# PEER gathers: the sums over rows of v, from both table stages to the last one alone

## The chip, the cores and the metric

One core of a Trainium2 chip runs the whole program. The metric is the device time of one execution in microseconds. The kernel before took 1464.52 us (median of three runs, 1464.1 to 1466.99).

## The reference, cut to what matters

The program computes two transformer blocks over 256 tokens of width 1024. The change touches only the last layer, `peer` (a product-key mixture of experts), whose table v is summed as follows:

```python
idx = ...                                  # (T, 8 heads, 16 picks): 128 of 16384 experts per token
g = softmax(top_s)
u_sel = take(u_tab, idx)                   # rows of u, 1024 floats each
h = einsum('bthkd,btd->bthk', u_sel, xb)   # 128 dot products per token
a = gelu(h) * g
y = einsum('bthk,bthkd->btd', a, take(v_tab, idx))   # 128 weighted rows of v per token
x = x + y
```

## The kernel before

The matmuls of all layers work through a list of weight blocks, `ORDER`, each 128 x 1024 floats (512 KB). SyncE fetches every block into `RAW`, a ring of four. The last 256 blocks are the two expert tables: 128 blocks of u (the **u stage**, `UP + c`, c from 0 to 127) and 128 blocks of v (the **w stage**, `WP + c`).

**Two ways to compute the layer.** Tokens 64 to 255 are dense: each goes against all 16384 experts. Tokens 0 to 63 are sparse: only their own 128 experts are fetched, each row by an indirect DMA. A gather takes one row for each of 128 partitions (64 tokens twice), so 64 gathers of u (`("u", j)`) and 64 of v (`("v", j)`) make the 128 picks of a token. Another 16 gathers of u (`("x", k)`) serve 16 of the dense tokens in the u stage.

**The u stage.** TensorE multiplies block c straight from `RAW` in plain float32 (`direct`, L1135, 16 matmul passes of 176 columns), and `gate_matmuls` adds twelve small bf16 matmuls behind 48 of the blocks, the quads. ScalarE takes the gelu of the block's result (`gelu`, L982), which TensorE waits for two blocks later (`pe.wait_ge(s_gel, c - 1)`), and VectorE multiplies by the gates (`gated`, `meet`, L1672). At c = 125 to 127 ScalarE and VectorE also make the first blocks of the w stage. The blocks WP and WP + 1 come into a spare buffer, `OHS` (L510), when the last quads are done, and their two transfers go out in SyncE's queue around block WP - 1.

**The w stage.** Block c is split into a high part `WH` (ScalarE, `high`, L678) and a low part `WL` (VectorE, `low`, L494). TensorE then makes ten matmuls of 512 columns with the activations `GG`. `WH` and `WL` have three buffers, so the engines work about two blocks ahead of TensorE: in step c of their loops they wait until TensorE is done with block c - 1, make `GG` for block c + 2 (ScalarE L1044 and L1045, VectorE L1672), and then split block WP + c + 2. SyncE fetches a block four further on once `WL` of the block in that place is made (`wait_low`).

**The gathers.** GpSimd issues all of them in one list, `TAKEN`, in that order: u gathers go to `UB` (L642) and v gathers to `VB` (L651), three buffers each (`NGET`). A gather waits until VectorE has used the buffer: `pool.wait_ge(s_dot, n - NGET + 1)` for u and `pool.wait_ge(s_vs, j - NGET + 1)` for v. VectorE turns a u row into a dot product (`dot`, L2304) and adds a v row to `YS` (`summed`, L1675 by way of `stt`). Before the first sum of each group of eight it multiplies gelu and gate (`weights`). Which steps of the loops hold them stands in two tables:

```python
TAKE_SLOT = {ROUTED + 1 + 85 * e // (N_SLOT - 1): TAKEN[EARLY_DOTS + e] for e in range(N_SLOT)}   # u stage
SUM_SLOT = {2 + 15 * (j - EARLY_SUMS) // 7: j for j in range(EARLY_SUMS, NSP)}                     # w stage
```

Ten dots are done ahead of step 39 of the u stage. The other 54 dots of u, the 16 of x and 8 sums (`EARLY_SUMS`) stand in 78 of the steps 40 to 125. From step 94 on every fourth of them is a sum (94, 98, 102, 107, 111, 116, 120, 125). The other 56 sums stand in the steps 2 to 119 of the w stage, seven in each fifteen. After the last one ScalarE moves half of `YS` (step 122) and VectorE adds the halves (step 124).

Of the kernel before, what the change touches and what calls it, by code (L numbers as in the profile page):

```python
# [113 lines left out]
NSP = 64  # L114
# [80 lines left out]
NGG = 3  # L195

EARLY_DOTS = 10
EARLY_SUMS = 8
TAKEN = [("u", j) for j in range(EARLY_DOTS)] + [("x", k) for k in range(NX)] + [("u", j) for j in range(EARLY_DOTS, 40)]
for _k in range(EARLY_SUMS):  # L200
    TAKEN += [("u", 40 + 3 * _k), ("u", 41 + 3 * _k), ("u", 42 + 3 * _k), ("v", _k)]
TAKEN += [("v", j) for j in range(EARLY_SUMS, NSP)]
N_SLOT = NSP + NX + EARLY_SUMS - EARLY_DOTS
TAKE_SLOT = {ROUTED + 1 + 85 * e // (N_SLOT - 1): TAKEN[EARLY_DOTS + e] for e in range(N_SLOT)}
# [2 lines left out]
DOTTED = {c: take for c, take in TAKE_SLOT.items() if take[0] != "v"}  # L207
X_DONE = max(c for c, take in DOTTED.items() if take[0] == "x")

SUM_SLOT = {2 + 15 * (j - EARLY_SUMS) // 7: j for j in range(EARLY_SUMS, NSP)}  # L210
GROUP = 8


# [52 lines left out]
def build(nc, wall, par, con, xt, rel, keys, utab, out):  # L266
    ctx = ExitStack()
    with ctx:
# [1401 lines left out]
        def vector_program(dve):  # L1670
# [6 lines left out]
            def low_if_mine(b):  # L1677
                if not low_on_pool(b) and b not in DIRECT:
                    low(dve, b)
# [688 lines left out]
            def summed(j):  # L2368

                if j % GROUP == 0:  # L2370
                    weights(j // GROUP)
                    dve.wait_ge(s_wgt, j // GROUP + 1)
                dve.wait_ge(d_v[j % NGET], 16 * (j // NGET + 1))
                if j == 0:
                    dve.wait_ge(s_xe, 2)
                    dve.wait_ge(s_zero, 2)
                else:
                    dve.wait_ge(s_vs, j)
                stt(YS[:, :], VB[:, j % NGET, :], AS[:, j:j + 1], YS[:, :], ALU.mult, ALU.add).then_inc(s_vs, 1)
# [27 lines left out]
            for c in range(127):  # L2407
                if 1 <= c < 126:
                    activations_low(c + 2)
                if WP + c + 2 < N_BLOCKS:  # L2410
                    low_if_mine(WP + c + 2)
                if c in SUM_SLOT:
                    summed(SUM_SLOT[c])
                if c == 124:
# [159 lines left out]
```

## Time and profile before

| | us |
|---|---|
| median of three runs | 1464.52 |
| the profiled execution | 1466.01 |
| its span | 1463.8 |
| TensorE busy in the span | 1440.5 (98%) |
| VectorE busy | 1128.2 (77%) |
| ScalarE busy | 773.2 (53%) |
| GpSimd busy | 342.2 (23%) |

A busy TensorE is one with a matmul in its pipe. The DMA share is the mean busy share of the core's 16 DMA engines, and it can come out a little over 1 in short stretches. A line number can be that of a helper (`mm`, `tt`, `stt`), so rows are told apart by the buffers that they name.

### The profile page before, as it was taken

The numbers are of one execution on the slowest core, as the hardware profiler recorded it, in microseconds if no ns is written. First come the engines' busy times: TensorE is split into PE (matmuls) and PEld (weight loads), VectorE is DVE, ScalarE is ACT, GpSimd is POOL, SyncE is SP. The second block draws the span as 40 slices with busy tenths as digits, with TensorE's granted clock in tenths as the row PEclk, the third lists the DMA queues.
The fourth block names the chain that finished last, engine by engine and source line by source line (L and its number), as shares of the span: only waits on it lengthen the run. The fifth ranks groups of instructions, "written<-read, shape, count | busy, mean of one in ns | idle before, by whom it ended". The sixth has DMA issues, their size and how long they took to land.

```text
span 1463.8 us, 26213 instructions
## 1 busy us (share of the span) xinstructions
PE 1440.5 (98%) x10046; PEld 1335.7 (91%) x10046; DVE 1128.2 (77%) x2197; ACT 773.2 (53%) x1583; POOL 342.2 (23%) x259
## 2 busy tenths in 40 slices
PE   6999999999999999999999999999999999999998
PEld 6999997789999988899999999999999988888886
DVE  6766678867666686877778797787788788888886
ACT  7555556666555556643455222444444466666665
POOL 1111112301111121201006112323333233333330
PEclk9999999999999999999999999999999999999999
DMA  5666656445665565454555579999999998999996
GB/s 189 194 193 189 188 174 236 151 140 167 187 188 188 183 198 183 140 154 144 171 175 159 164 262 346 343 343 353 362 368 365 341 326 319 337 336 331 320 339 202
DMA packets 98074, 353.06 MB, mean 241 GB/s; under 512 B 10904, under 2 KB 12192, under 8 KB 97952
## 3 DMA queue, kind: packets, MB, share of 16 engines
q1 hardware_dynamic: 77216, 275.90, 56.7%
q0 software_dynamic: 20736, 75.51, 14.0%
q8 instruction: 80, 1.31, 0.4%
q14 instruction: 42, 0.34, 0.1%
HBM read 350.32 MB, written 1.05 MB: 240 GB/s over the span
## 4 chain that ended last, share of the span: by engine, by line
PE 94%; DVE 2%; issue 1%; ACT 1%; POOL 1%; DMA 1%; SPq 0%; ACTq 0%; POOLq 0%; DVEq 0%
PE ps L1105 93%; DVE WL L494 1%; DMA RAW<-wall 1%; PE ps L1307 0%; PE ps L1326 0%; ACT HH L696 0%; POOL FS L587 0%; POOL NR L558 0%; DVE SQN L1672 0%; ACT SQN L685 0%; DMA XT<-xt 0%; POOL WH L567 0%; PE ps L1225 0%; DVE HL L1675 0%; DVE XT L1672 0%
## 5 line engine op out<-in xcount | busy, mean ns | idle before, releaser
L494 DVE TENSOR_TENSOR WL<-RAW,WH 128x1024 fp32r<-128x1024 f32 x359 | 440.7, 1228 | 163.3 <-ACT WH L678 154.4
L678 ACT ACTIVATE WH<-RAW 128x1024 fp32r<-128x1024 f32 x350 | 368.8, 1055 | 240.2 <-PE ps L1105 223.9
L1105 PE MATMUL ps<-XT,RAW 128*128 128x176 f32 x2048 | 317.8, 314 | 1.1 <-DMA RAW<-wall 0.6
L1105 PEld LDWEIGHTS ps<-XT,RAW 128*128 128x128 f32 x2048 | 305.6, 190 | 2.1 <-ACT BIG L976 0.9
L1105 PE MATMUL ps<-HH,WH 128*128 128x256 f32 x976 | 275.4, 282 | 0.8 <-DVE FP L1672 0.5
L1105 PE MATMUL ps<-HL,WH 128*128 128x256 f32 x976 | 272.6, 279 | 0.0
L1105 PE MATMUL ps<-HH,WL 128*128 128x256 f32 x976 | 272.4, 279 | 0.0
L1105 PE MATMUL ps<-WH,GG 128*128 128x512 f32 x768 | 261.9, 395 | 0.0
L1105 PE MATMUL ps<-WL,GG 128*128 128x512 f32 x512 | 202.0, 395 | 0.0
L1105 PEld LDWEIGHTS ps<-HH,WH 128*128 128x128 f32 x976 | 183.5, 188 | 2.2 <-DVE FP L1672 0.7
L1105 PEld LDWEIGHTS ps<-HL,WH 128*128 128x128 f32 x976 | 183.5, 188 | 0.0
L1105 PEld LDWEIGHTS ps<-HH,WL 128*128 128x128 f32 x976 | 183.6, 188 | 0.0
L1105 PEld LDWEIGHTS ps<-WH,GG 128*128 128x128 f32 x768 | 144.7, 188 | 34.0 <-issue 0.4
L651 POOL DMA_INDIRECT VB<-wall,IDXV x64 | 101.0, 1579 | 196.7 <-DVE YS L1675 189.2
L587 POOL TENSOR_TENSOR FS<-FS,RN 128x256 f32<-128x256 f32 x44 | 62.6, 1423 | 280.8 <-ACT FS L742 280.8
L1105 PEld LDWEIGHTS ps<-WL,GG 128*128 128x128 f32 x512 | 96.5, 188 | 22.4
L642 POOL DMA_INDIRECT UB<-utab,IDXU x64 | 66.5, 1040 | 169.4 <-DVE UB L2304 144.3
L1105 PE MATMUL ps<-FH,WH 128*128 128x256 f32 x352 | 98.4, 280 | 0.3 <-DVE WL L494 0.2
L1105 PE MATMUL ps<-FH,WL 128*128 128x256 f32 x352 | 97.8, 278 | 0.0
L1105 PE MATMUL ps<-FL,WH 128*128 128x256 f32 x352 | 97.8, 278 | 0.0
L2304 DVE SCALAR_TENSOR_TENSOR UB<-UB,XS 128x1024 f32<-128x1024 f32 x64 | 78.1, 1221 | 16.1 <-DMA UB<-utab,IDXU 12.6
L1105 PE MATMUL ps<-WH,HH 128*128 128x512 f32 (+1 forms) x208 | 84.7, 407 | 2.5 <-DVE WL L494 2.4
(298 smaller groups left out, 2418.6 us busy)
## 6 DMA issues: line engine op xcount, KB each, us to landing
RAW<-wall SPq DMA_DIRECT2D x508, 512.0 KB
B<-rel SPq DMA_DIRECT2D x4, 768.0 KB, 6.3
DEC<-con SPq DMA_DIRECT2D x4, 384.0 KB, 4.2
XT<-xt SPq DMA_DIRECT2D x4, 256.0 KB, 5.6
UB<-utab,IDXU POOLq DMA_INDIRECT x64
VB<-wall,IDXV POOLq DMA_INDIRECT x64
OHS<-wall SPq DMA_DIRECT2D x2, 512.0 KB, 8.4
WIN<-con SPq DMA_DIRECT2D x1, 768.0 KB, 8.6
```

Source lines behind the costliest of these rows:

```text
L494: ins = eng.tensor_tensor(wl, raw(b), wh.bitcast(F), ALU.subtract)
L587: pool.tensor_tensor(FS[:, j % 2, :], FS[:, j % 2, :], RN[:, :], ALU.mult).then_inc(s_srn, 1)
L642: pool.indirect_dma_start(UB[:, n % NGET, :], None, utab, bass.IndirectOffsetOnAxis(ap=at, axis=0)).then_inc(d_u[n % NGET], 16)
L651: pool.indirect_dma_start(VB[:, j % NGET, :], None, rows_of_wall, bass.IndirectOffsetOnAxis(ap=IDXV[:, j:j + 1], axis=0)).then_inc(d_v[j % ...
L678: act.activation(halves(b)[0], raw(b), ACT.Copy).then_inc(s_hi, 1)
L1105: return pe.matmul(o, l, r, start=start, stop=stop, skip_group_check=True)
L2304: dve.scalar_tensor_tensor(out=u, in0=u, scalar=1.0, in1=of, op0=ALU.mult, op1=ALU.mult, accum_out=to[:, j:j + 1]).then_inc(s_dot, 1)
```

## The change

The sums leave the u stage. `EARLY_SUMS` is 0 in place of 8; the u gathers 40 to 63, which stood three between two v gathers, now follow one another in `TAKEN`; and the 64 sums stand in the steps 2 to 119 of the w stage, seven in each thirteen.

```diff
-EARLY_SUMS = 8
+EARLY_SUMS = 0
 TAKEN = [("u", j) for j in range(EARLY_DOTS)] + [("x", k) for k in range(NX)] + [("u", j) for j in range(EARLY_DOTS, 40)]
 for _k in range(EARLY_SUMS):
     TAKEN += [("u", 40 + 3 * _k), ("u", 41 + 3 * _k), ("u", 42 + 3 * _k), ("v", _k)]
+TAKEN += [("u", j) for j in range(40 + 3 * EARLY_SUMS, NSP)]
 TAKEN += [("v", j) for j in range(EARLY_SUMS, NSP)]
 N_SLOT = NSP + NX + EARLY_SUMS - EARLY_DOTS
...
-SUM_SLOT = {2 + 15 * (j - EARLY_SUMS) // 7: j for j in range(EARLY_SUMS, NSP)}
+SUM_SLOT = {2 + 13 * j // 7: j for j in range(NSP)}
```

What follows from the tables: `N_SLOT` becomes 70, so 70 dots in place of 78 dots and sums spread over the steps 40 to 125. The last x dot moves from step 56 to 58, and the small steps that hang on it move with it. The last u dot moves from step 123 to 125, in the place of the eighth sum. The dots u59 to u62 stand at 120 to 123. The sums of the w stage start with j = 0 and stand in the steps 2, 3, 5, 7, 9, 11, 13, 15, 16, 18 and so on to 119; nine times two neighbouring steps both hold one (2 and 3, 15 and 16, up to 106 and 107), where before there was always a step between.

## Rows read from the trace of the kernel before

**Rows 1.** The page's busy times of the engines.
```profile
PE 1440.5 (98%) x10046; PEld 1335.7 (91%) x10046; DVE 1128.2 (77%) x2197; ACT 773.2 (53%) x1583; POOL 342.2 (23%) x259
```

**Rows 2.** Critical chain from 800 us on: start us, us, what.
```profile
896.94 7.64 DMA RAW<-wall
...
912.56 245.89 PE ps L1105 x1986
...
1158.93 300.17 PE ps L1105 x1296
```

**Rows 3.** Stretches, by core 0: us, busy us of each engine, PEclk, DMA share, GB/s.
```profile
1050.00:1100.00 50.00, 50.00 (x408) 49.48 (x407) 41.59 (x100) 22.82 (x92) 18.12 (x17) 1.00 1.00 371
...
1200.00:1250.00 50.00, 50.00 (x217) 40.55 (x216) 43.17 (x54) 30.98 (x64) 17.14 (x11) 1.00 0.90 316
1250.00:1300.00 50.00, 50.00 (x217) 40.46 (x216) 44.14 (x55) 33.08 (x67) 16.30 (x11) 1.00 0.96 344
```

**Rows 4.** The same view for GpSimd alone: share and GB/s in stretches of 2 us.
```profile
1146.00:1148.00 2.00, 1.39 (x1) 1.00 0.90 315
...
1152.00:1154.00 2.00, 0.00 (x0) 1.00 1.02 418
```

**Rows 5.** Timeline of the stage boundary: start us, us, instruction, idle before it.
```profile
1149.19 0.44 SPq L510 DMA_DIRECT2D OHS<-wall  x1
...
1157.56 1.06 ACT L678 ACTIVATE WH<-OHS 128x1024 fp32r<-128x1024 f32 x1 [1.16 <-DMA OHS<-wall]
...
1158.93 2.62 PE L1105 MATMUL ps<-XT,RAW 128*128 128x176 f32 x16 [0.49 <-ACT GT_ L982]
...
1161.27 0.52 PE L1105 MATMUL ps<-WH,GG 128*128 128x512 f32 x1
```

**Rows 6.** Timeline of GpSimd's gathers at the same boundary.
```profile
1141.75 0.94 POOL L642 DMA_INDIRECT UB<-utab,IDXU  x1 [1.60 <-DVE UB L2304]
1143.00 1.31 POOL L651 DMA_INDIRECT VB<-wall,IDXV  x1 [0.30 <-issue]
...
1145.86 1.54 POOL L651 DMA_INDIRECT VB<-wall,IDXV  x1 [0.30 <-issue]
1155.76 1.08 POOL L651 DMA_INDIRECT VB<-wall,IDXV  x1 [8.37 <-DVE YS L1675]
```

**Rows 7.** Groups by form on VectorE, 1165 to 1445 us: count, busy us, mean ns, idle.
```profile
L494 DVE TENSOR_TENSOR WL<-RAW,WH 128x1024 fp32r<-128x1024 f32 x122 | 149.3, 1224 | 33.9 <-ACT WH L678 32.7 <-issue 0.6
L1675 DVE SCALAR_TENSOR_TENSOR YS<-VB,AS,YS 128x1024 f32<-128x1024 f32 x56 | 71.7, 1280 | 0.2
```

**Rows 8.** Timeline of VectorE around a step with a sum, then one without.
```profile
1266.48 1.28 DVE L1675 SCALAR_TENSOR_TENSOR YS<-VB,AS,YS 128x1024 f32<-128x1024 f32 x1
1267.68 0.35 DVE L1672 TENSOR_TENSOR GG<-BIG,GG 128x192 fp32r<-128x192 f32 x1
1267.95 1.22 DVE L494 TENSOR_TENSOR WL<-RAW,WH 128x1024 fp32r<-128x1024 f32 x1
1269.08 0.35 DVE L1672 TENSOR_TENSOR GG<-BIG,GG 128x192 fp32r<-128x192 f32 x1
1269.99 1.23 DVE L494 TENSOR_TENSOR WL<-RAW,WH 128x1024 fp32r<-128x1024 f32 x1 [0.55 <-ACT WH L678]
```

**Rows 9.** ScalarE's waits, 1160 to 1464 us: total, times, longest.
```profile
ACT WH L678 <- DMA RAW<-wall: 15.3, 28, 1.4
```

**Rows 10.** Timeline of VectorE: `WL` of block WP + 35, then of block WP + 39.
```profile
1241.01 1.22 DVE L494 TENSOR_TENSOR WL<-RAW,WH 128x1024 fp32r<-128x1024 f32 x1
...
1250.58 1.23 DVE L494 TENSOR_TENSOR WL<-RAW,WH 128x1024 fp32r<-128x1024 f32 x1 [0.95 <-ACT WH L678]
```

**Rows 11.** Timeline of ScalarE: `WH` of block WP + 39, then the move of `YS`.
```profile
1249.49 1.06 ACT L678 ACTIVATE WH<-RAW 128x1024 fp32r<-128x1024 f32 x1 [1.40 <-DMA RAW<-wall]
...
1446.66 1.06 ACT L1093 ACTIVATE XS<-YS 64x1024 f32<-64x1024 f32 x1
```

## The prediction, made before the changed kernel ran

> **What bounds the kernel now.** I read the page's busy times first, then the chain of waits over the last 660 us, then the stretches of the two table stages, and last the timelines of each engine where the change puts or takes something. The page says that TensorE is busy for 1440.5 of 1463.8 us [rows 1], so 23 us at most are idle in the whole program. The chain says where those are not: from 912.56 us on it is TensorE's own work for 245.89 us, then a short step aside, then TensorE again for 300.17 us until the last matmul [rows 2]. The stretches show TensorE busy for all of each 50 us in both stages, at the full clock (1.00, so 2.4 GHz), while VectorE has 41.59 us of work in the fullest one of the u stage and 43.17 to 44.14 us in the w stage [rows 3]. So every step that the change moves is beside TensorE's chain. It can win only TensorE's waits in that part, and it can lose by making one.
>
> There are two such waits. One stands before the chain's piece at 912.56: the transfer in the chain at 896.94 [rows 2], at a point where no v gather has been issued (the first one waits for the last x dot). The change doesn't touch it. The other is 0.49 us at the stage boundary, at 1158.93, where TensorE waits for a gelu that ScalarE does late, because ahead of it in ScalarE's order stands the split of block WP, and that waited 1.16 us for its transfer [rows 5].
>
> **The change part by part.**
>
> *Removed from the u stage: 8 sums and 8 gathers.* Eight sums of 1.28 us [rows 7] are 10.2 us of VectorE's time and 4.2 MB of transfers. TensorE waits for neither there, so the worth is 0. That holds with all of the old load: 1050 to 1100 us moved 371 GB/s at a DMA share of 1.00 without a wait of TensorE [rows 3]. The bounds are 0 and -0.49 us, the boundary wait, which I count below.
>
> *Moved within the u stage: dots and their gathers.* They go from 78 slots in 85 blocks to 70, so most stretches thin out (one in 1.09 blocks to one in 1.21). Only behind step 93 do the u dots get denser, 21 of them in 32 steps before and 26 now, while all gathers together fall from 29 to 26. A gather of u then has three slots of about 1.21 x 2.8 us (a block with its share of quads, 245.89 us over some 88 blocks [rows 2]), which is 10.2 us less the dot. VectorE has some 10 us of each 50 idle there [rows 3] and takes a late row from that. Cost 0.
>
> *Kept at the boundary: step 125.* A dot (u63) takes the place of a sum, 1.22 us for 1.28. Cost 0. The last gathers move, though. Before, GpSimd issued the last u gather at 1141.75 and three v gathers from 1143.00 to 1145.86, and one more at 1155.76 [rows 6]. Now u63 can go only when u60 is dotted, in step 121 and not 119, some 5 us later; v0, v1 and v2 have free buffers and follow at once, till about 1151. The fourth isn't issued at all before step 2 of the w stage. So the same four transfers meet the two of `OHS`, the first at 1149.19 [rows 5], more closely, where the engines already run full at 418 GB/s (1152 to 1154), after 315 GB/s at 1146 to 1148 [rows 4]. One transfer of 512 KB at 418 GB/s is 1.25 us. The block that ScalarE waits for has 8.4 us from its issue to 1157.56 [rows 5]. If two transfers more get ahead of it, it lands 2.5 us later, and TensorE waits 2.5 us more; if the missing one of 1155.76 and the thinner load before let it land 0.5 us sooner, the 0.49 us go. The bounds are -0.5 and +2.5 us. I take +0.2: two queues that share the engines leave SyncE's half as it was, and the number in flight is the same.
>
> *Added to the w stage, VectorE's part.* Seven sums in thirteen blocks in place of seven in fifteen. From start to start a sum takes 1.20 us (1266.48 to 1267.68), `GG` 0.27 and `WL` 1.13 to 1.14 [rows 8]. A block of TensorE is 300.17 us less the last u block of 2.34, over 128: 2.327 us [rows 2, 5]. Per block VectorE needs 1.41 + 7/15 x 1.20 = 1.97 us now and 1.41 + 7/13 x 1.20 = 2.06 us then, 88% of the block. In a step with a sum it needs 2.61 us and runs 0.28 us over; in two such steps in a row 0.57 us over, and the next step, 0.92 us under, takes it back. `WL` is ready 1.6 to 1.9 us before TensorE wants it when its transfer is on time (1270.0 + 1.23 against block WP + 48, wanted at 1161.27 + 48 x 2.327 = 1273.0) [rows 5, 8]. After a pair some 1.3 us are left. Cost 0 by itself.
>
> *Added to the w stage, the transfers.* Here the cover is thin. ScalarE waited 28 times for `RAW`, 15.3 us together, 1.4 us at the most [rows 9]. At the worst one the split began at 1249.49 [rows 11], `WL` was done at 1250.58 + 1.23 = 1251.81 [rows 10], and TensorE wanted it at 1161.27 + 39 x 2.327 = 1252.02. It was 0.2 us from a stall. That transfer had been asked for when `WL` of block 35 was done at 1241.01 + 1.22 = 1242.23 [rows 10], so it took 7.3 us. What the w stage asks for is 512 KB x (1 + 7/15) per 2.327 us, 330 GB/s (the stretches show 316 and 344 [rows 3]); it becomes 512 KB x (1 + 7/13), 347 GB/s. That is 5% more, under the 371 that the u stage took for 50 us and well under 418 [rows 3, 4]. The u stage gives the nearest comparison: a block asked for when TensorE leaves the one four before it has three blocks, 3 x 2.8 = 8.4 us; here it has the 7.0 us to ScalarE's usual start and the 1.6 us of slack behind, 8.6 us. With 371 GB/s nothing stalled there. So the bounds are 0 (as the u stage) and, if every one of the 28 late blocks becomes later by a whole further transfer, 28 x (0.55 + 1.25 - 1.65) = 4.2 us, where 0.55 is the mean of now and 1.65 the usual slack. I take +0.5 us, two or three short stalls in 128 blocks, nearer to the u stage's row.
>
> The Trainium skill, "DMA: Bandwidth & Descriptors", section "Where 436 GB/s comes from", speaks against the change: it says that for loads from HBM the HBM side binds, at about 358 GB/s per core. By that the w stage would come within 3% of its ceiling, bursts would hardly drain, and the sum would go by the upper bound, +4.2 us, in place of +0.5. This trace doesn't agree with it: 371 GB/s over 50 us and 418 over 2 us [rows 3, 4].
>
> *The end.* The last sum stays in step 119. ScalarE moves `YS` at 1446.66 [rows 11], over 12 us ahead of the last matmul, so a sum that is late by a gather costs nothing. Cost 0.
>
> *The sum.* +0.2 and +0.5 make +0.7 us. Against the profiled execution, a span of 1463.8 us and 2.2 us around it (1466.01), that is 1466.7 us. The three timed runs have their median 1.5 us below the profiled one, so the forecast is 1464.52 + 0.7 = 1465.2 us. About 0.2%, 2.9 us, is what a measurement of this kernel can tell from no change, so I forecast no change.
>
> **The rivals.**
>
> *A, the late transfer starves TensorE in the w stage (slower).* The place is `RAW` before ScalarE's split, the point from which it decides is a transfer 1.65 us later than ScalarE's usual start, and the price is 4.2 us, or 1468.7 us. For it: the 0.2 us that were left at block 39, and that a late `WL` also asks late for the block four further on, as block 35 did for block 39. Pairs of sums make that oftener, nine times. Against it: the u stage's 371 GB/s, and that one stall of TensorE gives all the following blocks their slack back. In the worst form the engines carry no more than the w stage's own 344 GB/s [rows 3] with every queue full; then 128 blocks stretch by 1%, 2.6 us, on top.
>
> *B, the boundary (slower, under the bound).* The burst of v0 to v2 keeps back the two `OHS` blocks: +2.5 us and the 0.5 of the w stage, 1467.5 us. For it: the share is 1.02 already there [rows 4]. Against it: one gather fewer behind 1155, and a half share for each queue.
>
> *C, faster.* All of TensorE's waits in reach go: -0.49 us, 1464.0 us. For a gain of over 2.9 us TensorE's own pace would have to change, and it has none of its idle time there to give.
>
> *D, the change doesn't do what it says.* The list and the tables hold each of the 64 sums once, so I leave this one no chance of its own.
>
> **How the numbers follow.** The forecast has 0.62, A 0.19, B 0.12, C 0.07. The predicted time is the forecast's 1465.2 us. Timed runs of one kernel lie 3 us apart (1464.1 to 1466.99), a median of them less. The range runs from 1463.4 (C less the spread of a median) to 1468.8 (A without its worst form). Slower by over 0.2%, above 1467.4, is A and nearly no B: a quarter of A and half of B stay below it, and some of the forecast's spread comes above, 0.20 in all. Faster by over 0.2%, below 1461.6, is only an accident of measurement, 0.03. The rest is 0.77.
>
> **What would show it.** In the w stage of the changed profile: TensorE busy for all of each 50 us (the forecast) or with waits for VectorE's `WL` (A). ScalarE's waits for `RAW` grow from 15.3 us to some 20 to 30; over 45 us, or one longer than 1.7 us, speaks for A. GB/s from some 331 to 347 in the middle of the stage. VectorE some 2 us more of each 50. At the boundary: TensorE's wait for the gelu between 0 and 1 us; over 2 us is B. In the u stage: TensorE as before, and fewer GB/s behind 1050 us. The forecast is wrong if TensorE's busy share falls in any stretch that the chain shows as its own, or if a matmul's pace changes.

## The result, and the profile after

The changed kernel is slower: 1469.03 us against 1466.3 us in the same sessions (medians of 20 runs each), a ratio of 1.0022 with a 95% interval from 1.0015 to 1.003. That is 3.2 us (0.0022 x 1466.3), with bounds of 2.2 and 4.4; the two medians by themselves are 2.7 us apart. The profiled execution has a span of 1465.7 us against 1463.8.

The forecast was +0.7 us. The direction and most of the size are those of rival B, the stage boundary, with its +3.0 us. The forecast's absolute time, 1465.2 us, lies 3.8 us under the measured one. Of these 1.8 us are not the change's: it started from the 1464.52 us of three runs, and the same kernel has 1466.3 us here.

First the stretches of the changed kernel (columns as in [rows 3]). The u stage and its end, then two of the w stage:

```profile
1050.00:1100.00 50.00, 50.00 (x414) 49.44 (x413) 39.62 (x97) 22.32 (x90) 17.11 (x14) 1.00 0.94 337
1100.00:1150.00 50.00, 49.09 (x396) 48.44 (x394) 39.54 (x93) 18.80 (x74) 18.22 (x17) 1.00 0.95 334
1150.00:1200.00 50.00, 48.20 (x233) 40.88 (x232) 37.84 (x53) 28.02 (x62) 13.23 (x9) 1.00 0.89 328
1200.00:1250.00 50.00, 50.00 (x217) 40.54 (x216) 44.91 (x57) 31.58 (x65) 20.35 (x12) 1.00 0.96 349
1250.00:1300.00 50.00, 50.00 (x215) 40.04 (x214) 45.98 (x58) 32.31 (x65) 21.45 (x11) 1.00 0.94 341
```

The w stage came out as worked out: 349 and 341 GB/s where 316 and 344 stood, VectorE 1.7 and 1.8 us busier, and TensorE busy for all of it. What is gone is gone ahead of it, between 1100 and 1200 us. ScalarE's waits from 1160 us on say the same. Here are the ones for transfers (as [rows 9]):

```profile
ACT WH L679 <- DMA RAW<-wall: 14.4, 25, 1.4
...
ACT WH L679 <- DMA OHS<-wall: 1.8, 1, 1.8
```

25 late blocks in place of 28, with 5% more bytes asked for. The price is at the boundary. The timeline of it (as [rows 5]):

```profile
1149.02 0.44 SPq L511 DMA_DIRECT2D OHS<-wall  x1
...
1151.04 0.33 SPq L515 DMA_DIRECT2D RAW<-wall  x1
...
1157.97 1.06 ACT L679 ACTIVATE WH<-OHS 128x1024 fp32r<-128x1024 f32 x1 [1.84 <-DMA OHS<-wall]
...
1159.96 2.62 PE L1106 MATMUL ps<-XT,RAW 128*128 128x176 f32 x16 [1.79 <-DMA RAW<-wall]
1161.07 1.06 ACT L679 ACTIVATE WH<-OHS 128x1024 fp32r<-128x1024 f32 x1 [1.84 <-DMA OHS<-wall]
```

TensorE now waits 1.79 us, not for a gelu but for the last block of u itself: `RAW` was asked for at 1151.04 and its block started at 1159.96, 8.9 us later. `OHS` took 8.9 us (1149.02 to 1157.97) in place of 8.4. GpSimd's timeline shows what may be in the way (as [rows 6]):

```profile
1146.15 0.94 POOL L643 DMA_INDIRECT UB<-utab,IDXU  x1 [1.77 <-DVE UB L2305]
1147.39 1.51 POOL L652 DMA_INDIRECT VB<-wall,IDXV  x1 [0.30 <-issue]
1149.21 0.95 POOL L652 DMA_INDIRECT VB<-wall,IDXV  x1 [0.31 <-issue]
1150.46 0.94 POOL L652 DMA_INDIRECT VB<-wall,IDXV  x1 [0.30 <-issue]
1171.66 1.95 POOL L652 DMA_INDIRECT VB<-wall,IDXV  x1 [20.26 <-DVE YS L1676]
```

The last u gather and three of v go out within 5 us, as before, but 4.4 us later, so that they straddle the first `OHS` transfer (1149.02) and the last of them goes out just ahead of the second (1151.41). The reader should also see the gap behind them: GpSimd issues nothing for 20 us, since v3 waits for the first sum. None of these v rows was wanted before that sum started, at 1170.11.

There is one more wait in the u stage, which the kernel before doesn't have there. VectorE waited 3.91 us for a u row, and a quad's one-hots came late:

```profile
1107.74 1.23 DVE L2305 SCALAR_TENSOR_TENSOR UB<-UB,XS 128x1024 f32<-128x1024 f32 x1 [3.91 <-DMA UB<-utab,IDXU]
```
```profile
1111.51 0.85 PE L1106 MATMUL ps<-OHS 128*128 128x128 bf16 x12 [0.91 <-DVE OHS L1673]
```

So there were three candidates: the boundary (theory 1), the closer dots behind step 93 (theory 2), and the pace of the w stage (theory 3).

### The profile page after: what moved, and what is told of

Read it like the earlier page. It is cut to its first block, busy times and chain, and to the rows that moved or that the text cites. A ratio compares the mean times of both kernels' runs of the same rounds, so it can differ in the third digit from the quotient of the medians.

```text
span 1465.7 us, 26213 instructions
## 1 busy us (share of the span) xinstructions
PE 1439.0 (98%) x10046; PEld 1332.5 (91%) x10046; DVE 1126.1 (77%) x2197; ACT 772.5 (53%) x1583; POOL 357.5 (24%) x259
## 4 chain that ended last, share of the span: by engine, by line
PE 91%; DMA 3%; DVE 2%; issue 1%; ACT 1%; POOL 1%; SPq 0%; DVEq 0%; ACTq 0%; POOLq 0%
PE ps L1106 90%; DMA RAW<-wall 2%; DVE WL L495 1%; DMA UB<-utab,IDXU 1%; PE ps L1308 0%; POOL FS L588 0%; PE ps L1327 0%; ACT HH L697 0%; POOL NR L559 0%; DVE SQN L1673 0%; DMA XT<-xt 0%; ACT SQN L686 0%; ACT WH L679 0%; POOL WH L568 0%; PE ps L1226 0%
## 5 line engine op out<-in xcount | busy, mean ns | idle before, releaser
L652 POOL DMA_INDIRECT VB<-wall,IDXV x64 | 111.9, 1749 | 172.1 <-DVE YS L1676 167.9
```

Of the source, the lines that this page charges most:

```text
L652: pool.indirect_dma_start(VB[:, j % NGET, :], None, rows_of_wall, bass.IndirectOffsetOnAxis(ap=IDXV[:, j:j + 1], axis=0)).then_inc(d_v[j % ...
```

## The experiments

All ratios are to the kernel before, run beside them, from 11 or 12 runs of each kernel and 33 to 35 of the kernel before. The quotients of the medians differ from them by up to 0.0008 (1.0004 in place of 0.9996 for the pace alone), so a difference of a few ten-thousandths between two runs says nothing. The number that reads the boundary best, free of what happened earlier, is the time from the issue of the first `OHS` transfer to the first matmul of the w stage. It is 12.08 us before (1149.19 to 1161.27 [rows 5]) and 13.28 us in the changed kernel's profile (1149.02 to 1162.30). It is one execution for each run, and it varies from one to the next, as the runs will show.

**Holding the first v gather.**

```diff
                 if j == 0:
                     pool.wait_ge(s_dot, U_TURN["x", NX - 1] + 1)
+                    pool.wait_ge(d_first[1], 16)
```

> The changed kernel, with the first v gather held until the second spare block (OHS) has landed, so that v0 to v2 go out some 14 us later, behind the stage boundary. Theory 1 (the boundary: v0 to v2 collide with the two OHS transfers and with the RAW of block 127; TensorE waited 1.8 us there in the changed profile against 0.5 before): TensorE's wait at the boundary goes to 0 to 0.5 us and the ratio to the kernel before falls from 1.0022 to about 1.0012. Theory 2 (the u dots behind step 93 stand closer, a late u gather holds up the one-hots of a quad; 0.9 us in the changed profile): the ratio stays about 1.002. Theory 3 (RAW comes late in the w stage at 347 GB/s): it stays about 1.002, with waits of TensorE in the w stage.

Measured: ratio 0.9986 (0.9973 to 0.9998), 11.25 us between the two events. The whole loss is gone, and a little more. The timelines of its boundary (`d_first[1]` is the semaphore of the second `OHS` transfer):

```profile
1147.97 0.43 SPq L511 DMA_DIRECT2D OHS<-wall  x1
...
1154.98 1.05 ACT L680 ACTIVATE WH<-OHS 128x1024 fp32r<-128x1024 f32 x1
1157.37 1.05 ACT L680 ACTIVATE WH<-OHS 128x1024 fp32r<-128x1024 f32 x1
```
```profile
1157.19 0.94 POOL L653 DMA_INDIRECT VB<-wall,IDXV  x1 [11.14 <-DMA OHS<-wall]
```

ScalarE doesn't wait: `OHS` is there within 7.0 us (1147.97 to 1154.98). I had expected to win back 1 us in 3, and the ratio fell by some 5 us; the effect is larger than the one profile of the changed kernel had shown. This run has the closer dots and the w stage of 64 sums too, so theories 2 and 3 had little left.

**The dots in their old steps.** The u and x dots stand in the 70 steps of the old 78 that held them, and the eight steps of the sums stay empty; the w stage is the changed one.

```diff
-TAKE_SLOT = {ROUTED + 1 + 85 * e // (N_SLOT - 1): TAKEN[EARLY_DOTS + e] for e in range(N_SLOT)}
+TAKE_SLOT = {ROUTED + 1 + 85 * e // 77: _OLD[EARLY_DOTS + e] for e in range(78) if _OLD[EARLY_DOTS + e]}
```

`_OLD` is the list `TAKEN` of before with nothing in the places of v0 to v7.

> The changed kernel, with the u and x dots back in the steps that they had before (the eight steps of the sums stay empty); the w stage is the changed one, 64 sums at seven in thirteen. u63 is dotted in step 123 and the v gathers go out some 5 us earlier again, so this undoes what theories 1 and 2 blame and keeps what theory 3 blames. Theories 1 and 2: ratio 1.000 (0.9990 to 1.0008), no wait of TensorE over 0.5 us from 912 us on. Theory 3: ratio about 1.002 and waits of TensorE for WL in the w stage.

Measured: ratio 0.9996 (0.9985 to 1.0007), 12.00 us between the events. Its last four gathers go out from 1142.35 to 1146.08, as before. So the 64 sums of the w stage cost nothing that can be measured, against theory 3: the loss of 3.2 us lies outside the interval, and TensorE doesn't wait anywhere in the w stage of this profile. Its one wait from 912 us on is 0.36 us at the boundary.

**The pace alone.** In the kernel before:

```diff
-SUM_SLOT = {2 + 15 * (j - EARLY_SUMS) // 7: j for j in range(EARLY_SUMS, NSP)}
+SUM_SLOT = {2 + 13 * (j - EARLY_SUMS) // 7: j for j in range(EARLY_SUMS, NSP)}
```

> The kernel before with one edit: its 56 sums of the w stage stand seven in thirteen steps (2 to 104) in place of seven in fifteen. Theory 3 (the pace of the w stage costs the time): ratio 1.002, with TensorE waiting for WL between 1170 and 1405 us. Theories 1 and 2: ratio 1.000, no wait of TensorE there.

Measured: ratio 0.9996 (0.9986 to 1.0007), 12.68 us between the events, and no wait of TensorE from 1165 us on. Theory 3 has fallen twice. This profile also has two waits for late one-hots in its u stage (1.4 us together). It has the dot steps of before, so such a wait isn't a mark of the closer dots. And at the boundary, which the edit doesn't touch, TensorE waited 1.20 us for a block of u at 1155.32, where the first profile of the kernel before has 0.49: with the burst where it was before, the slack is used up too, by an amount that varies.

**The pace undone.** The changed kernel without the gathers and sums of v0 to v7, so that eight terms are missing from the sparse tokens (not shown: the other gathers and sums count their buffers and semaphores from v8):

```diff
-TAKEN += [("v", j) for j in range(EARLY_SUMS, NSP)]
+TAKEN += [("v", j) for j in range(8, NSP)]
...
-SUM_SLOT = {2 + 13 * j // 7: j for j in range(NSP)}
+SUM_SLOT = {2 + 15 * (j - 8) // 7: j for j in range(8, NSP)}
```

> The changed kernel with the w stage at the old pace: the gathers and sums of v0 to v7 are left out altogether (eight terms of the 128 picks are missing from the sparse tokens), the other 56 stand in the steps that they had before. The u stage and the boundary are the changed ones. Theories 1 and 2: ratio about 1.002, waits of TensorE in the u stage and at the boundary as in the changed profile. Theory 3: ratio 1.000 or below.

Measured: ratio 1.0022 (1.001 to 1.0034), 16.61 us between the events (1151.91 to 1168.52). The same loss with the w stage of before.

**Holding in the kernel before.** v8 is the first gather that only the w stage wants.

```diff
+                if j == EARLY_SUMS:
+                    pool.wait_ge(d_first[1], 16)
```

> The kernel before, with v8 (the first gather that only the w stage wants) held until the second spare block (OHS) has landed; v8 to v10 go out at about 1157 us in place of 1145 to 1156. Theory 1 (gathers in flight around 1149 to 1158 us keep back OHS and block 127): the kernel before pays there too, so the ratio is about 0.9988, and TensorE's wait of 0.5 us at the boundary and ScalarE's wait for OHS (1.2 us) are gone. Theory 4 (the holding run is faster than the kernel before because its u stage has 70 slots, not 78, and the boundary is worth only what the change lost): ratio 1.000.

Measured: ratio 0.9994 (0.9985 to 1.0003), 11.24 us between the events. In the profile TensorE's 0.49 us and ScalarE's 1.2 us are gone, as theory 1 has it. I had expected 0.9988 of it; the gain of 0.9 us is half of that and lies within the interval of none, so theory 4 isn't excluded by the times alone.

**Releasing with the `OHS` issue.** In the changed kernel, ahead of v0:

```diff
+                    pool.wait_ge(s_bt, NQUAD - 1)
```

> The changed kernel, with v0 to v2 released at the event at which SyncE issues the first OHS transfer (the 47th quad done, 1149 us), so 1149 to 1152 in place of 1147 to 1151. Theory 1 (it is the coincidence that costs): as bad as the changed kernel or worse, ratio 1.0022 to 1.004. If what counts were only that the v gathers wait a little, so that the u gathers land first, it would fall between, 1.000 to 1.001.

Measured: ratio 1.0019 (1.0008 to 1.0029), 14.73 us between the events. But the edit held nothing back, as the timeline shows:

```profile
1140.90 0.85 PE L1107 MATMUL ps<-OHS 128*128 128x128 bf16 x12
...
1148.48 1.51 POOL L653 DMA_INDIRECT VB<-wall,IDXV  x1 [0.30 <-issue]
...
1150.11 0.43 SPq L511 DMA_DIRECT2D OHS<-wall  x1
```

The event is the 47th quad, and that was done with the matmuls of 1140.90. SyncE issues `OHS` over 8 us later, since a `RAW` block that goes out only at 1149.73 stands ahead of it in its program. So v0 went out 1.63 us ahead of `OHS`, as in the changed kernel (1147.39 and 1149.02). My expectation took the quad to be done at 1149, which is wrong, and its question, what a short delay does, stays untested. The run is one more set and one more profile of the changed kernel's order.

**The old dot steps and the hold.** Both edits together.

> The run with the old dot steps, with the first v gather held until the second OHS block has landed. Against the holding run with the changed steps (ratio 0.9986) only the steps of the dots differ. Theory 1 alone: 0.9986 as well (0.998 to 0.999). Theory 4 (the thinner slots of the changed u stage are what gains): 0.9996, as with the old dot steps and no hold. Theory 2 (the closer dots behind step 93 cost): lower than 0.9986.

Measured: ratio 0.999 (0.9981 to 0.9999), 11.25 us between the events. Like the holding run with the closer dots (0.9986), so no run shows the cost of theory 2. The old steps gain as much as the new ones, against theory 4, though the 0.9996 that it expected here still lies within the interval. Against the run with the old steps and no hold, the profile has lost the waits at the boundary (12.00 to 11.25 us).

**The changed kernel again.**

> The changed kernel once more, on the chip of these runs, and a second profile of it. Theory 1: ratio 1.0022, and again a wait of TensorE of over 1 us at the stage boundary, with ScalarE waiting for OHS. If the wait of 1.8 us in the first profile was an accident, the second shows about 0.5 us as the kernel before does.

Measured: ratio 1.002 (1.0009 to 1.003), 15.73 us between the events (1150.60 to 1166.33). The wait was no accident, and this profile shows more than the first. Its timeline has a wait of 2.27 us:

```profile
1159.98 1.06 ACT L679 ACTIVATE WH<-OHS 128x1024 fp32r<-128x1024 f32 x1 [2.27 <-DMA OHS<-wall]
...
1162.47 4.29 PE L1106 MATMUL ps<-XT,RAW 128*128 128x176 f32 x16 [2.27 <-DMA RAW<-wall]
1163.56 1.06 ACT L679 ACTIVATE WH<-OHS 128x1024 fp32r<-128x1024 f32 x1 [2.32 <-DMA OHS<-wall]
...
1166.33 0.68 PE L1106 MATMUL ps<-WH,GG 128*128 128x512 f32 x1
```

and behind it the 16 matmuls of the block took 4.29 us in place of 2.62. The stretches around it (columns as in [rows 3]) give the reason in the granted clock:

```profile
1160.00:1162.00 2.00, 0.21 (x2) 0.00 (x0) 0.93 (x1) 1.25 (x2) 0.00 (x0) 1.00 1.02 418
...
1163.00:1164.00 1.00, 1.00 (x7) 1.00 (x6) 0.00 (x0) 0.44 (x1) 0.00 (x0) 0.63 1.04 426
1164.00:1165.00 1.00, 1.00 (x5) 1.00 (x4) 0.35 (x1) 0.62 (x1) 0.00 (x0) 0.50 1.00 410
1165.00:1166.00 1.00, 1.00 (x5) 1.00 (x5) 0.88 (x1) 0.00 (x0) 0.00 (x0) 0.50 0.39 160
1166.00:1167.00 1.00, 1.00 (x5) 0.95 (x5) 0.00 (x0) 0.20 (x1) 0.00 (x0) 0.67 0.12 49
1167.00:1168.00 1.00, 1.00 (x6) 0.79 (x5) 0.34 (x1) 0.69 (x5) 0.00 (x0) 1.00 0.64 82
```

The stall cost 2.27 us and then 1.5 us again, 1162.47 to 1166.33 being 3.86 us where a block takes 2.34.

**One, two, and none in the burst.** The changed kernel with the hold at v1, or at v2 (`j == 2`), and the first holding run once more:

```diff
+                if j == 1:
+                    pool.wait_ge(d_first[1], 16)
```

> The changed kernel, with v0 going out as in it (about 1148 us) and v1 and v2 held until the second OHS block has landed. So far, from the issue of the first OHS transfer to the first matmul of the w stage: 11.25 us with none in the burst (three profiles), 13.3 to 16.6 us with three (four profiles). Theory 1 with a price per gather: one third of the loss, 12 to 12.7 us, ratio about 0.9998. If a burst only costs once it is long enough (a threshold), it is like none: 11.3 us, 0.9988.

> The changed kernel, with v0 and v1 going out as in it and v2 held until the second OHS block has landed. Price per gather: two thirds of the loss, 13 to 14 us between the two events, ratio about 1.001. Threshold: as one, or as three, and nothing between.

> The run with the first v gather held, once more: its ratio of 0.9986 had an interval from 0.9973 to 0.9998. Theory 1: 0.999 (0.998 to 1.000), 11.25 us between the two events.

| v gathers between the last u gather and the second `OHS` transfer | ratio | 95% interval | us between the two events |
|---|---|---|---|
| 0 (two sets) | 0.9986, 0.9989 | 0.9973 to 0.9998, 0.9979 to 0.9998 | 11.25, 11.25 |
| 1 | 0.9994 | 0.9986 to 1.0003 | 11.24 |
| 2 | 1.0007 | 0.9998 to 1.0017 | 13.38 |
| 3 (two sets, the run whose release held nothing, and the run without v0 to v7) | 1.0022, 1.002, 1.0019, 1.0022 | 1.0015 to 1.003, 1.0009 to 1.003, 1.0008 to 1.0029, 1.001 to 1.0034 | 13.28, 15.73, 14.73, 16.61 |

The ratio rises with each gather; the intervals of neighbouring rows overlap, those of none and three don't. The profiles show one hidden altogether and the second not, which is between my two expectations: there is slack for one.

**Fetching earlier, without a hold.** v0, v1 and v2 are issued behind u44, u48 and u52, since their buffers are free from the last x dot on.

```diff
                 if kind == "v":
-                    gather_v(j)
+                    if j >= 3:
+                        gather_v(j)
                 else:
                     gather_u(kind, j)
+                    if kind == "u" and j in (44, 48, 52):
+                        gather_v((j - 44) // 4)
```

> The changed kernel without any hold: v0, v1 and v2 are issued behind the u gathers 44, 48 and 52, some 20 to 50 us ahead of the boundary, into buffers that are free from the last x dot on. The same bytes and the same steps of VectorE, and no gather of v near the OHS transfers. Theory 1: as the holding run, 11.25 us between the two events and ratio 0.999. If it were the count of the gathers in the w stage or the hold itself that matters, it stays near 1.002. The cost could be in the u stage: a u gather behind each of them is 1 us later in GpSimd's queue, so up to +0.5 us.

Measured: ratio 0.9989 (0.998 to 0.9997), 11.24 us between the events. The three gathers go out at 1081.49, 1095.63 and 1110.24, earlier than I had reckoned. Nothing is held, nothing is left out, and all 64 sums are in the w stage, so neither their count nor a wait made the loss. This run and the holding one beat the changed kernel clearly, and the kernel before by about 0.1%, with intervals that end just under 1. One mark of rival A does show in this profile, a wait of TensorE of 0.4 us for a `WL` of the w stage, the only one in any profile. ScalarE's longest wait for `RAW` is 1.99 us there (at 1265.76), over the 1.65 us that the prediction had named as the slack, and 1.4 in the kernel before.

To see what the three gathers (512 KB each) do there, here are the stretches of GpSimd's view (as [rows 4]), the changed kernel first and then the one that fetches earlier:

```profile
1150.00:1154.00 4.00, 1.10 (x2) 1.00 1.02 394
1154.00:1158.00 4.00, 0.00 (x0) 1.00 1.02 409
1158.00:1162.00 4.00, 0.00 (x0) 1.00 1.02 417
```
```profile
1150.00:1154.00 4.00, 0.00 (x0) 1.00 1.04 370
1154.00:1158.00 4.00, 0.00 (x0) 1.00 0.96 379
1158.00:1162.00 4.00, 0.00 (x0) 1.00 0.90 309
```

In the changed kernel the engines stay full until TensorE's wait is over. In the other they have caught up by 1158.

## Why the prediction was wrong

*What bounds the kernel*: right. TensorE's chain is the time, and all that the change did was to make it wait.

*The u stage, removed sums at 0*: right. The stretch at 1050 fell from 371 to 337 GB/s and gave TensorE nothing.

*The dots moved within the u stage at 0*: not refuted by any run. The one late row of the profile cost 0.91 us, but the run with the closer dots and no burst (0.9986) is no slower than the run with the old steps and no burst (0.999), and the run at the new pace with the old steps has two such waits of its own. In all, two of the nine profiles with the closer dots show a wait of TensorE for one-hots (0.9 and 0.7 us), and one of the five with the old steps. A cost of a few tenths would not show in the ratios.

*The boundary*: this is the step that failed. I worked out the move of the four gathers rightly ("some 5 us later"; they were 4.4), bounded it by -0.5 and +2.5 us, and took +0.2 with the reason that "two queues that share the engines leave SyncE's half as it was, and the number in flight is the same". The first half of the reason is wrong, and the second is no reason. An `OHS` block took 7.0 to 7.4 us at most (the start of ScalarE's split) in the kernels with no v gather beside it and 8.9 to 10.6 us with three (in the changed kernel's two profiles 1149.02 to 1157.97 and 1152.99 to 1163.56). And the number in flight was the same, but not over the same time: before, the four gathers began 7.4 us ahead of SyncE's two extra transfers, with the engines at 315 GB/s just before [rows 4, 6]; after, the first began 2.9 us ahead (1146.15 to 1149.02) and the last behind the first of the two.

The term measured +3.2 us against the kernel before (1.0022), since with the old order at the boundary and all else changed the ratio is 0.9996. The profiles agree: with the burst of three the time between the two events is 13.28 to 16.61 us, 15.1 in the mean of four, and with the order of before 12.00 to 12.68 us, 12.3 in the mean of three, 2.8 us less. In them TensorE's longest wait at the boundary went from 0.36, 0.49 and 1.20 to 1.79, 2.26, 2.27 and 2.32 us, and in three of the four the clock took 1.0 to 1.6 us more. My upper bound of two transfers' worth was therefore too low by the clock's part, which I had not counted at all. How the engines divide their time between the two queues no run shows; what is shown is that the `OHS` blocks and the last u block land later. I also read the 0.49 us of TensorE and the 1.16 us of ScalarE there [rows 5] as a wait to be lost, when they said that this was the one place of both stages where the slack was already used up.

*The w stage, VectorE*: right, 1.7 and 1.8 us more of each 50, where I had said some 2.

*The w stage, transfers, +0.5 us*: too high, so far as the profiles tell. TensorE has no wait in the w stage of the changed kernel in either profile, and ScalarE's waits for `RAW` did not grow (15.3 us before, 14.4 after). Two kernels with the new pace came out at 0.9996, but their intervals would hide 0.5 us. The 0.4 us of the run that fetches earlier show that the cover was as thin as I had said. The comparison with the u stage's 371 GB/s was sound, and rival A's price of 4.2 us is refuted.

*The bandwidth*: the changed kernel moved 417 GB/s over 4 us, and its w stage asked for 347 without a wait of TensorE. The Trainium skill, "DMA: Bandwidth & Descriptors", section "Where 436 GB/s comes from", gives about 358 GB/s for loads from HBM; the measurement stays against it.

*Against rival B as I had priced it*: place and mechanism are B's, 3.0 us forecast and 3.2 measured, but the closeness is partly luck: 0.5 of the 3.0 were for the w stage, where nothing was lost, the wait grew by less than 2.5 us, and the clock came on top. The sign that I had set for B, a wait of over 2 us, came in the second profile (2.27) and not in the first (1.79). I gave B 0.12 and set it under the 0.2% bound, though by its own price it stood just over it (1467.5 against 1467.4).

What stays open: whether taking the sums out of the u stage is worth anything by itself (theory 4). The kernel before with the burst held (0.9994, 0.9985 to 1.0003) and the changed kernel with it held (0.9986 and 0.9989) can't be told apart.

## What to carry to other kernels

When a step is moved, follow the transfers that it releases to the moment at which they go out, and look for another burst there; equal bytes and an equal mean rate say nothing when both meet at a stage boundary. A wait of a few tenths on the bounding engine in the profile before marks the place without slack: price a change there at its upper bound. If a queue issues in program order and a buffer has long been free, fetch early or hold back until the critical transfers have landed; here either brought the changed kernel from 1.0022 to 0.9989 of the kernel before (the first set of the holding run: 0.9986). Check in the trace that a hold really holds: one here waited for an event that was long past.

## What the runs showed of the hardware that was not expected

TensorE's granted clock fell after a short wait. In the second profile of the changed kernel it waited 0.23 us, worked for one block, waited 2.27 us, and was then at 0.50 (1.2 GHz) from 1164 to 1166, with work in its pipe all the time, and at 1.00 (2.4 GHz) again from 1167. The run whose release held nothing (a wait of 2.26 us, the only one since 912 us) and the one without v0 to v7 (0.63 us, one block, and 2.32 us) show the same, the blocks behind taking 3.75 and 4.22 us on the timeline. In the first profile of the changed kernel the wait was 1.79 us and the clock stayed at 1.00; its block took 2.62 us. The Trainium skill, "TensorE: Matmul & The Clock Gate", Part 1, says that the clock is either full or half and goes by how busy TensorE has been; the two levels are what these rows show.

The run whose release held nothing shows it in stretches of 2 us:

```profile
1160.00:1162.00 2.00, 0.49 (x3) 0.52 (x4) 1.48 (x2) 0.19 (x1) 0.00 (x0) 1.00 1.03 422
1162.00:1164.00 2.00, 2.00 (x12) 2.00 (x11) 0.43 (x1) 1.06 (x1) 0.00 (x0) 0.71 1.01 414
1164.00:1166.00 2.00, 2.00 (x8) 1.81 (x7) 1.14 (x2) 0.41 (x2) 0.00 (x0) 0.50 0.23 94
1166.00:1168.00 2.00, 2.00 (x10) 1.62 (x9) 0.84 (x2) 1.46 (x3) 0.00 (x0) 0.94 0.71 238
```
